# The mixers' first norm taken out of the matmul's input and put into its eviction, with the residual's centring on GpSimd

## What is computed

```python
h  = x * ALPHA + 0.5 * swiglu(x, ffn1_w_gate, ffn1_w_up, ffn1_w_down)   # D_FF 2816
mu = mean(h); var = mean(square(h - mu))
n  = (h - mu) * rsqrt(var + EPS) * ln1_g + ln1_b                        # ln1
proj = n @ w_in                     # 20 blocks of 128 columns in the kernel
z, xbc, dt, fq, fk, fv, f, cq, ckv, k_rope = split(proj)
y  = concat(ssd_mixer(z, xbc, dt), fox_mixer(fq, fk, fv, f), mla_mixer(cq, ckv, k_rope))
h2 = n * ALPHA + y @ w_out          # then ln2, ffn2, ln3
```

## Time and profile before

| what | us |
|---|---|
| median of 3 runs | 2019.23 (2018.91 to 2019.35) |
| the profiled execution's own time | 2020.61 |
| its span | 2018.9 |
| granted TensorE clock, mean over the span | 0.998 |
| TensorE busy | 1999.1 |
| VectorE busy | 1419.5 |
| ScalarE busy | 1010.3 |
| GpSimd busy | 115.5 |

### The profile page before, as it was taken

How to read it: one execution, slowest core, us unless ns; L and a number is a source line. 1 busy time by engine, 2 the same in 40 slices (tenths; PEclk the granted TensorE clock), 3 DMA queues, 4 the chain that set the end, 5 groups by cost and what they waited for, 6 DMA issues and landing times.

```text
span 2018.9 us, 42417 instructions
## 1 busy us (share of the span) xinstructions
PE 1999.1 (99%) x16236; PEld 1951.8 (97%) x16236; DVE 1419.5 (70%) x2565; ACT 1010.3 (50%) x1497; POOL 115.5 (6%) x151
## 2 busy tenths in 40 slices
PE   9999999999999999999999999999999999999998
PEld 9999889999999998899998999999999999999998
...
GB/s 256 183 200 156 105 105 126 183 171 193 155 169 178 198 122 126 84 176 188 187 182 196 199 206 168 139 134 188 187 201 170 198 194 194 138 124 188 186 206 148
...
## 3 DMA queue, kind: packets, MB, share of 16 engines
...
...
HBM read 341.25 MB, written 1.05 MB: 170 GB/s over the span
## 4 chain that ended last, share of the span: by engine, by line
PE 93%; DVE 4%; ACT 1%; DVEq 1%; issue 0%; DMA 0%; ACTq 0%; SPq 0%; POOL 0%
PE ps L565 29%; PE ps L567 29%; PE ps L566 29%; DVE w_lo L1875 1%; ACT w_hi L1231 1%; DVE plain L1966 0%; PE ps L1092 0%; PE ps L914 0%; PE ps L903 0%; PE ps L852 0%; PE ps L1034 0%; PE ps L1129 0%; DMA raw<-in_w_up 0%; PE ps L789 0%; PE ps L819 0%
## 5 line engine op out<-in xcount | busy, mean ns | idle before, releaser
L1875 DVE TENSOR_TENSOR w_lo<-raw,w_hi 128x1024 fp32r<-128x1024 f32 (+1 forms) x582 | 748.7, 1313 | 158.7 <-ACT w_hi L1231 158.2
L1231 ACT ACTIVATE w_hi<-raw 128x1024 fp32r<-128x1024 f32 (+1 forms) x582 | 635.2, 1122 | 231.2 <-PE ps L567 219.0
L565 PE MATMUL ps<-x_hi,w_lo 128*128 128x256 f32 (+2 forms) x2416 | 693.1, 287 | 7.7 <-DVE x_lo L1942 5.1
L567 PE MATMUL ps<-x_hi,w_hi 128*128 128x256 f32 (+2 forms) x2416 | 685.2, 284 | 0.0
L566 PE MATMUL ps<-x_lo,w_hi 128*128 128x256 f32 (+2 forms) x2416 | 682.3, 282 | 0.0
L565 PEld LDWEIGHTS ps<-x_hi,w_lo 128*128 128x128 f32 x2416 | 455.5, 189 | 19.7 <-issue 14.2
L566 PEld LDWEIGHTS ps<-x_lo,w_hi 128*128 128x128 f32 x2416 | 455.3, 188 | 0.8
L567 PEld LDWEIGHTS ps<-x_hi,w_hi 128*128 128x128 f32 x2416 | 455.7, 189 | 0.0
L565 PE MATMUL ps<-hid_hi,w_lo 128*128 128x256 f32 (+1 forms) x1536 | 435.6, 284 | 0.7 <-DVE hid_lo L2053 0.4
L566 PE MATMUL ps<-hid_lo,w_hi 128*128 128x256 f32 (+1 forms) x1536 | 434.1, 283 | 0.0
L567 PE MATMUL ps<-hid_hi,w_hi 128*128 128x256 f32 (+1 forms) x1536 | 433.5, 282 | 0.0
...
## 6 DMA issues: line engine op xcount, KB each, us to landing
...
```

The lines of the kernel that those rows point to most:

```text
L565: mm(dst, w_lo[:, j, cols], xa, start=first, stop=False)
L567: return mm(dst, w_hi[:, j, cols], xa, start=False, stop=last)
L1231: fn(w_hi[:, j, c], raw[:, j, c], ACT.Copy).then_inc(hi_done, 1)
L1875: v.tensor_tensor(w_lo[:, j, c], raw[:, j, c], w_hi[:, j, c].bitcast(F32), ALU.subtract)\
```

## The change

For ln1 of both first blocks, the mixer's projection runs on the uncentred residual:

- x_hi and x_lo are made of h times gain, without the mean. Chunks 0 to 6 are split in the last turn of ffn1's `down`, chunk 7 behind it (`before_mixer_down` on ScalarE and VectorE, which takes the place of `down` or `level_down` there and of `layer_norm`). The squares are of the uncentred chunks, as the residuals come.
- Of the two extra columns the second now holds the gain, so column 273 of each block is the product of weights and gain.
- TensorE runs the mean at step 2 and the second moment at step 4 of the first pair. ScalarE makes `neg_mean` and its square, VectorE the variance (`level_norm`).
- `scale(i)` has three operations: the copy, neg_mean times column 273 plus the block, and the product with rstd. There are 20 in each layer.
- GpSimd's sums of chunks and of squares are interleaved (`level_sums`). Its `residual` adds neg_mean (eight) and multiplies by rstd (eight); gain and bias are applied by ScalarE (`residual(k)`, eight Identity operations, between the steps of the mixer).

```diff
-            def variance(l, n):
-
-                mean_square(l * 3 + (n + 1), ln_sq, l * (3 * KD) + (n * KD + KD), T1 if n == 0 else OUT_T[l])
...
-                first_pair(turn0, event, 0, N1)
-                variance(l, 0)
+                first_pair(turn0, event, 0, N1, None,
+                           {2: lambda: mean(l * 3, T1), 4: lambda: level_variance(l * 3, T1)})
                 blocks(2, 4)
...
                 down(q, t0 + SEC1["ffn1"] + UP_T, r0, T1)
-                mean(r0, T1)
                 pe.wait_ge(prm_in, l * 16 + 16)
                 last_heads = mixer1(l, t0 + SEC1["in"], l * 2 + 1)
...
-            def layer_norm(norm, gain, bias, next_turn, T):
-                fn(x_hi[:, :, T:T + 2], par(P1, bias, 0, KD).rearrange("p (k a) -> p k a", a=1).broadcast_to([P, KD, 2]),
-                   ACT.Copy)
-                for k in range(KD):
-                    act.wait_ge(centered, (norm + 1) // 3 * KD + (k + 1))
-                    high(P1, gain, k, T, T + 2)
-                    fn(pj[:, KD + k, 0:T], h[:, k, T1 - T:T1], ACT.Square).then_inc(ln_sq, 1)
-                second_pair(next_turn, 1)
-                root(norm, T, "eps1")
+            def before_mixer_down(turn0, norm, T):
+                for m in range(KD):
+                    last = m == KD - 1
+                    split_next(turn0 + m // 2, m % 2, W_NARROW if last else W_WIDE)
+                    if last:
+                        for n, name in enumerate(("ln1b", "ln1g")):
+                            fn(x_hi[:, :, T + n:T + n + 1], par(P1, name, 0, KD).rearrange("p (k a) -> p k a", a=1), ACT.Copy)
+                        for k in range(KD - 1):
+                            high(P1, "ln1g", k, T, T + 2)
+                        second_pair(turn0 + DOWN_T, 0)
+                        load_log_exp()
+                        act.wait_ge(resid_ready, norm * KD + (KD + CREDIT))
+                        high(P1, "ln1g", KD - 1, T, T + 2)
+                    level_square(norm, m, T)
...
+                def residual(*chunks):
+                    for k in chunks:
+                        act.wait_ge(h_scaled, l * KD + (k + 1))
+                        fn(h[:, k, :], h[:, k, :], ACT.Identity, scale=par(P1, "ln1g", k), bias=par(P1, "ln1b", k))\
+                            .then_inc(h_ready, 1)
...
                 weights(11)
                 bias(8)
                 seed(4)
+                residual(0)
                 weights(12)
                 bias(9)
                 seed(5)
+                residual(1)
                 decay_pair(3)
                 weights(13)
                 bias(10)
+                residual(2)
...
                 weights(20)
+                residual(6, 7)
...
-                down(t0 + SEC1["ffn1"] + UP_T, r0, False, r0, T1)
                 act.wait_ge(prm_in, l * 16 + 16)
-                layer_norm(r0, "ln1g", "ln1b", t0 + SEC1["in"], T1)
+                before_mixer_down(t0 + SEC1["ffn1"] + UP_T, r0, T1)
+                level_norm(r0, t0 + SEC1["in"], T1)
...
                 lo_unit(next_turn, 1, 1, W_NARROW)
-                dve.wait_ge(neg_ready, LEVEL_NORM[norm] + 1)
-                dve.wait_ge(square_mean, LEVEL_NORM[norm] + 1)
+                dve.wait_ge(neg_ready, norm + 1)
+                dve.wait_ge(square_mean, norm + 1)
                 v.tensor_tensor(std[:, 1, 0:T], ps[:, 7, 0:T], std[:, 1, 0:T], ALU.subtract)
...
-                def centre(k):
-                    v.tensor_tensor(h[:, k, T1 - T:T1], h[:, k, T1 - T:T1], ps[:, 6, 0:T], ALU.subtract)\
-                        .then_inc(centered, 1)
-
-                dve.wait_ge(mean_ready, norm + 1)
-                centre(0)
-                centre(1)
-
-                dve.wait_ge(xh_ready, norm // 3 * KD + 1)
-                v.tensor_tensor(x_lo[:, :, T:T + 2],
-                                par(P1, bias, 0, KD).rearrange("p (k a) -> p k a", a=1).broadcast_to([P, KD, 2]),
-                                x_hi[:, :, T:T + 2].bitcast(F32), ALU.subtract)
-                for k in range(KD):
-                    low(norm // 3, P1, gain, k, T, T + 2)
-                    if k + 2 < KD:
-                        centre(k + 2)
-                lo_unit(next_turn, 1, 1, W_NARROW)
-                root(norm)
+            def before_mixer_down(l, turn0, T, gains=None, offsets=None):
+
+                for m in range(KD):
+                    last = m == KD - 1
+                    split_next(turn0 + m // 2, m % 2, W_NARROW if last else W_WIDE)
+                    c = h[:, m, T1 - T:T1]
+                    if gains:
+                        v.tensor_tensor(c, c, neg_mean[:, 0:T], ALU.add)
+                        dve.drain()
+                        v.scalar_tensor_tensor(out=c, in0=c, scalar=gains[:, m:m + 1], in1=rstd[:, 0:T],
+                                               op0=ALU.mult, op1=ALU.mult)
+                        dve.drain()
+                        v.tensor_scalar(c, c, offsets[:, m:m + 1], ALPHA, ALU.add, ALU.mult)
+                    if last:
+                        dve.wait_ge(xh_ready, l * KD + 1)
+                        for n, name in enumerate(("ln1b", "ln1g")):
+                            col = slice(T + n, T + n + 1)
+                            v.tensor_tensor(x_lo[:, :, col], par(P1, name, 0, KD).rearrange("p (k a) -> p k a", a=1),
+                                            x_hi[:, :, col].bitcast(F32), ALU.subtract)
+                        for k in range(KD - 1):
+                            low(l, P1, "ln1g", k, T, T + 2)
+                    dve.drain()
+                    dve.wait_ge(unit_used, turn0 * 4 + (2 * m + 2 + START))
+                    if gains:
+                        v.scalar_tensor_tensor(out=c, in0=ps[:, 4 + m % 2, 0:T], scalar=0.5, in1=c,
+                                               op0=ALU.mult, op1=ALU.add).then_inc(resid_ready, 1)
+                    else:
+                        resid(ALPHA, m, 4 + m % 2, T)
+                low(l, P1, "ln1g", KD - 1, T, T + 2)
+                lo_unit(turn0 + DOWN_T, 1, 0, W_NARROW)
...
                 def scale(i):
 
                     dve.wait_ge(unit_used, turn0 * 4 + (i + 1 + START))
-                    v.tensor_copy(wblk[:, i:i + 1], ps[:, i % IN_BANKS, T1:T1 + 1])
-                    v.tensor_tensor(pj[:, i, :], ps[:, i % IN_BANKS, 0:T1], rstd[:], ALU.mult).then_inc(proj_scaled.sem, 1)
+                    block = ps[:, i % IN_BANKS, :]
+                    v.tensor_copy(wblk[:, i:i + 1], block[:, T1:T1 + 1])
+                    v.scalar_tensor_tensor(out=pj[:, i, :], in0=neg_mean[:], scalar=block[:, T1 + 1:T1 + 2],
+                                           in1=block[:, 0:T1], op0=ALU.mult, op1=ALU.add)
+                    dve.drain()
+                    v.tensor_tensor(pj[:, i, :], pj[:, i, :], rstd[:], ALU.mult).then_inc(proj_scaled.sem, 1)
 
...
                 if l == 0:
                     up(q, t0 + SEC1["ffn1"], T1)
-                    down(t0 + SEC1["ffn1"] + UP_T, ALPHA, T1)
+                    dve.wait_ge(prm_in, l * 16 + 16)
+                    before_mixer_down(l, t0 + SEC1["ffn1"] + UP_T, T1)
                 else:
                     level_up(q, t0 + SEC1["ffn1"], LEVEL_UP[q], T1)
-                    level_down(t0 + SEC1["ffn1"] + UP_T, T1, kept[:, 0:KD], kept[:, KD:2 * KD])
-                dve.wait_ge(prm_in, l * 16 + 16)
-                layer_norm(r0, "ln1g", "ln1b", t0 + SEC1["in"], T1)
+                    dve.wait_ge(prm_in, l * 16 + 16)
+                    before_mixer_down(l, t0 + SEC1["ffn1"] + UP_T, T1, kept[:, 0:KD], kept[:, KD:2 * KD])
+                level_norm(r0, t0 + SEC1["in"], T1)
                 dve.wait_ge(consts_in, 16)
                 mixer1(l, t0 + SEC1["in"])
                 dve.wait_ge(h_ready, l * KD + (KD + START))
...
-            def residual(l, gain, bias, T):
+            def residual(l):
                 pool.wait_ge(x_ready, (l * 2 + 1) * KD + KD)
                 pool.wait_ge(std_ready, l * 3 + 1)
                 for k in range(KD):
-                    nc.gpsimd.tensor_tensor(h[:, k, T1 - T:T1], h[:, k, T1 - T:T1], rstd[:, 0:T], ALU.mult)
+                    nc.gpsimd.tensor_tensor(h[:, k, :], h[:, k, :], neg_mean[:], ALU.add)
                 pool.drain()
                 for k in range(KD):
-                    nc.gpsimd.tensor_scalar(h[:, k, T1 - T:T1], h[:, k, T1 - T:T1], par(P1, gain, k), par(P1, bias, k),
-                                            ALU.mult, ALU.add).then_inc(h_ready, 1)
+                    nc.gpsimd.tensor_tensor(h[:, k, :], h[:, k, :], rstd[:], ALU.mult).then_inc(h_scaled, 1)
 
             pool.nop().then_inc(h_ready, START)
 
...
-                residual_sums(l * 3, T1)
-                layer_norm_sums(l * 3, T1)
-                residual(l, "ln1g", "ln1b", T1)
+                level_sums(l * 3, T1)
+                residual(l)
```

14 lines of the change are left out of this document (6 added, 8 removed).

## The result

| | before | changed |
|---|---|---|
| median of the runs, us | 2019.98 (16 runs) | 2023.3 (16 runs) |
| lowest and highest, us | 2018.91, 2021.0 | 2021.55, 2025.95 |
| ratio, with its 95% interval | | 1.0017 (1.0009 to 1.0025) |
| span of the profiled execution, us | 2018.9 | 2021.9 |

The change makes the kernel 3.3 us **slower**, 0.17%. The interval leaves no doubt of the sign, though it is within the 0.2% that I had called no change. The forecast was −1.75 us, and the upper end of the range, 2022.0, is passed.

What follows compares the result with a forecast made beforehand. TensorE was taken as the bound, busy 1999.1 of 2018.9 us. Of 6.05 us saved at the joins, 0.6 a layer survives, plus 0.55 from the clock: −1.75 us, 2017.5 us; 8-in-10 range 2014.3 to 2022.0.

Steps and rivals of the forecast that it cites:

- The join: From the end of ffn1's `down` to the unit behind the mixer's first pair: 2.75 us saved in layer 0, 3.30 in layer 1.
- The ln3 form: The existing join at ln3, with uncentred chunks straight behind `down` and mean slipped in at step 2: 8.39 us, taken as pattern.
- The eviction: VectorE's eviction of each projection block: three operations at 1.00 us instead of two at 0.42, +0.58 for each of 20 blocks.
- With everything shifted against GpSimd's pass, up to both may be spared: Two weight operations beside GpSimd's residual, each lengthened by 0.5 us, may escape it: upper end of a layer's gain 1.4 us.
- the ledger: VectorE's chain in layer 0's mixer up to the row maxima: gain −0.2 to +0.3 us, widened to 1.4; 0.6 a layer taken.
- rival 2: GpSimd's two-tensor passes lengthen VectorE's products by 0.18 to 0.53 us, at most 1.0; net loss 17 in 100.
- L815: TensorE's `decay_rows` (L819 before the change) waiting for VectorE's L2238 in the mixer: some tenths of a us forecast.
- Token rows: VectorE's rows in the mixer that ScalarE's decay pair waits for: 1.18 us earlier.
- The maxima: VectorE's last row maxima, needed by TensorE for att_s(1): end 0.07 to 0.56 us later than now.
- The clock: TensorE's granted clock at layer 1's join, which fell to the 1.2 GHz level, stays up without the idle: 0.55 us gained.
- rival 3: TensorE's clock falls at new waits at L903 in both layers, 0.55 us each: 2018.6 us; 15 in 100.
- Behind att_s(1): Later part of the mixer: VectorE has idle time, evictions 12 to 19 fit there and cost nothing, no new waits.

Runs made afterwards that it cites:

- e1_psum: Changed kernel with one edit: the eviction's centring writes back to PSUM and the product with rstd reads it there; 2019.74 us, 0.9997 of before.
- the late version: Changed kernel with GpSimd's residual started only once unit 12 is done, ScalarE's residual operations later too; 2017.78 us, 0.9987 of before.

## Why the prediction failed

By its own steps:

- **The join**: right in kind, 6.05 us forecast and 6.98 measured. The ln3 form, taken as the pattern, takes 8.39 us and this one 7.93; why was not looked into. The work put into `down`, costed at nothing, cost nothing: TensorE is 1.7 us behind the trace of before at 141 us, where `down` begins, and 1.7 at its end (0.25 at both in `e1_psum`).
- **The eviction**: 1.00 us forecast; undisturbed it takes 218.53 − 217.55 = 0.98. Right. That it is paid up to L899 and not behind it was right too, as the third operation alone in the kernel before showed (+5.9 us, all but some 0.7 up to L903).
- **"With everything shifted against GpSimd's pass, up to both may be spared"** is the step that failed. I took the disturbance for something that stays at two weight operations or goes, and so widened the ledger by 1.05 us to the good side. It went the other way: the passes lie over 16 us of VectorE's work, the products have become liable to it, and the second pass disturbs the row sums more than gain and bias did (2.74 us in three operations instead of 2.15). The rows held this: rival 2 named the mechanism and its bounds of 0.18 to 0.53 us, and its price a product was 0.24 on average (1.2 us over five). But I had it as a rival and left it out of the sum, and counted only the products in it, not L2239 to L2244 and w_lo, which together are as large. By the ledger the chain up to L2238 was to be 4.08 − 1.74 − 0.58 = 1.76 us earlier, and it was 0.92; TensorE was to be 0.6 us earlier behind L903 in each layer, and it was 0.9 later. These 1.5 us twice are 3.0 of the 5.05 us between the forecast of −1.75 and the +3.3. Some 1.5 more are the clock (0.55 of gain that was forecast and about 1 of loss by the estimate above), and 0.4 the out projection of layer 1.
- **L815**: forecast some tenths, measured 2.2. Here the ledger was not even carried through: with L2238 1.76 us earlier and TensorE 2.75, its own numbers give 0.5 + 1.0 = 1.5 us. The other 0.7 is the term above (0.8) and the larger join (0.7), less the 0.8 that TensorE had waited at L760 before, a wait that the prediction does not have. Token rows 1.18 us earlier was forecast; measured from the end of `down` they come at 30.5 us instead of 30.8, 0.3 earlier. The maxima were to be 0.07 to 0.56 us later and were 1.3 later; both are off by 0.8 us or more, by this same term.
- **The clock**: forecast +0.55 us of gain, with rival 3 at 0.55 us of loss per fall. Both sized it from the fall at a join, where VectorE set the pace. Behind L815 it costs 1.5 us on the spot; in the changed kernel later waits hide 1.0 of it, in the kernel before with the longer second pass nothing did. The gain at the join came too, so in the trace the two cancel. But over the runs the mean clock was lower than before, 0.9971 instead of 0.9983, where it was to be higher. The longer waits at L815 are the likely reason; which waits made it fall in the executions without a trace is not recorded.
- **Behind att_s(1)** no new waits were forecast, and none of size came; the largest loss is 0.4 us at the out projection of layer 1.

Rival 2 is what happened in kind, with part of rival 3; rival 2 had 17 in 100. That its figure of 2022.8 lies so near the measured 2023.3 is luck: it stands for 0.53 us on each of five products, and the products lost 0.24 on average. The rest came from the operations that it left out and from the clock.

The Trainium skill's page "SBUF — State Buffer" (section "SBUF: two separate sides") has the pair of ports shared by VectorE and GpSimd as an exclusive lock held for a whole instruction. These runs agree in more than the first trace did: no single VectorE operation that I looked at was lengthened by more than 0.64 us (w_lo from 1.22 to 1.86, in the late version), less than GpSimd's undisturbed 0.77, as it must be if an operation waits for at most the rest of one; GpSimd's own operations grew by 1.0, less than a w_lo; and reading one operand from PSUM ended it. The whole 1.0 us that I had derived from the rule was wrong for want of GpSimd's undisturbed time.

What stays open is why some operations under GpSimd's passes were not lengthened at all (the products of blocks 1 and 3 at 0.44 in the changed kernel, w_lo of unit 6 at 1.28 in `e1_psum`): the phase of the two engines was not tried. Nor was it tried when a wait of some 2 us makes the clock fall and when not.
